# A quarter of each expert's down weights multiplied in f32 from the raw buffer, in a mixture-of-experts layer

## The reference, cut to what matters

```
gu    = xblk @ w_gu[e] + b_gu[e]          # w_gu[e]: 1024 x 2048, f32
x_glu = min(gu[:, :F], 7);  x_lin = clip(gu[:, F:], -7, 7)
act   = x_glu * sigmoid(1.702 * x_glu) * (x_lin + 1)
y     = act @ w_down[e] + b_down[e]       # w_down[e]: 1024 x 1024, f32
```

## Time and profile before

| | us |
|---|---|
| median of 3 runs | 1267.36 (1266.95 to 1268.4) |
| the profiled execution | 1267.78 |
| its span in the trace | 1266.0 |
| PE busy | 1160.1 (92%) |
| DVE busy | 1128.3 (89%) |
| ACT busy | 924.4 (73%) |
| POOL busy | 509.2 (40%) |

### The profile page before, as it was taken

One profiled execution on the slowest core, in us unless ns is written; L12 is line 12 of the kernel. 1 busy time (PEld: TensorE's weight loads), 2 busy tenths in 40 slices (PEclk: granted clock), 3 DMA queues, 4 the chain that ended last, 5 costly groups with the idle time before them and its releaser, 6 DMA issues.

```text
span 1266.0 us, 39786 instructions
## 1 busy us (share of the span) xinstructions
PE 1160.1 (92%) x17462; PEld 894.8 (71%) x17463; DVE 1128.3 (89%) x849; ACT 924.4 (73%) x819; POOL 509.2 (40%) x69
## 2 busy tenths in 40 slices
PE   5999999789999999999999999999999999999984
PEld 2455544777777777777777777777888777777741
DVE  5742454789999999999999999999999999999988
ACT  5332432579888888888888888888888888888852
POOL 0120300006666666666665551111166666622400
PEclk9999999799999999999999999999999999999998
DMA  9609331699999999999999999999999999999986
GB/s 350 218 20 353 126 134 58 229 371 378 420 416 416 418 413 417 418 418 417 416 417 414 419 418 418 414 418 413 415 416 419 417 411 420 418 412 409 418 324 255
DMA packets 73254, 458.07 MB, mean 362 GB/s; under 512 B 10076, under 2 KB 10588, under 8 KB 23632
## 3 DMA queue, kind: packets, MB, share of 16 engines
q1 hardware_dynamic: 68480, 445.30, 86.5%
q0 software_dynamic: 3472, 8.21, 1.7%
q10 hardware_dynamic: 1152, 2.19, 0.5%
HBM read 443.26 MB, written 24.77 MB: 370 GB/s over the span
## 4 chain that ended last, share of the span: by engine, by line
PE 44%; DVE 29%; issue 17%; DMA 6%; ACT 2%; DVEq 0%; SPq 0%; ACTq 0%; POOLq 0%
DVE ring L399 20%; PE ps L420 15%; PE ps L456 10%; PE ps L1093 8%; PE ps L1194 4%; PE ps L413 3%; DMA ring<-in_w_down_dram 2%; DMA arena<-in_w_down_dram 1%; DVE arena L492 1%; ACT ring L396 1%; DVE arena L486 1%; DVE arena L489 1%; DMA ring<-in_w_gu_dram 1%; DVE arena L501 1%; DVE arena L495 1%
## 5 line engine op out<-in xcount | busy, mean ns | idle before, releaser
L478 POOL DMA_INDIRECT planes<-arena,slot_row x31 | 484.2, 15619 | 586.8 <-ACT arena L508 586.8
L399 DVE SCALAR_TENSOR_TENSOR ring<-ring 128x2048 f16<-128x2048 f32 x290 | 657.5, 2315 | 15.0 <-ACT ring L396 14.7
L396 ACT ACTIVATE ring<-ring 128x2048 f16<-128x2048 f32 x290 | 543.1, 1905 | 46.4 <-DMA ring<-in_w_gu_dram 22.9
L420 PE MATMUL ps<-arena,ring 128*128 128x88 f16 x12288 | 505.1, 205 | 46.2 <-issue 27.8
L420 PEld LDWEIGHTS ps<-arena,ring 128*128 128x128 f16 x12288 | 489.2, 100 | 55.9 <-issue 43.2
L456 PE MATMUL ps<-ring,arena 128*88 128x512 f16 x1536 | 338.0, 379 | 5.6 <-DVE arena L501 2.6
L456 PEld LDWEIGHTS ps<-ring,arena 128*88 128x88 f16 x1536 | 181.4, 120 | 148.6 <-issue 6.0
L399 DVE SCALAR_TENSOR_TENSOR ring<-arena,ring 128x2048 f16<-128x2048 f32 x94 | 214.4, 2316 | 0.9 <-ACT ring L396 0.9
L396 ACT ACTIVATE ring<-arena 128x2048 f16<-128x2048 f32 x94 | 178.0, 1904 | 12.4 <-DMA arena<-in_w_down_dram 6.5
L413 PE MATMUL ps<-arena 128*128 128x88 f16 x2048 | 94.2, 207 | 10.9 <-issue 7.6
L413 PEld LDWEIGHTS ps<-arena 128*128 128x128 f16 x2048 | 86.6, 101 | 12.0 <-issue 11.9
(11 more groups left out here) (153 smaller groups left out, 592.7 us busy)
## 6 DMA issues: line engine op xcount, KB each, us to landing
ring<-in_w_gu_dram SPq DMA_DIRECT2D x194, 1024.0 KB, 11.9
ring<-in_w_down_dram SPq DMA_DIRECT2D x96, 1024.0 KB, 12.1
arena<-in_w_gu_dram SPq DMA_DIRECT2D x62, 1024.0 KB, 12.5
arena<-in_w_down_dram SPq DMA_DIRECT2D x32, 1024.0 KB, 11.7
ring<-in_w_in_dram SPq DMA_DIRECT2D x4, 2048.0 KB, 12.4
ring<-planes SPq DMA_DIRECT2D x6, 1024.0 KB, 10.1
ring<-in_w_out_dram SPq DMA_DIRECT2D x2, 2048.0 KB, 8.5
arena<-in_x_dram SPq DMA_DIRECT2D x4, 512.0 KB, 11.6
```

The source lines that it names most:

```text
L396: return act.activation(split_of(slot)[:, 0, :], raw(r), ACT.Copy, scale=SCALE_W)
L399: return dve.scalar_tensor_tensor(split_of(slot)[:, 1, :], raw(r), SCALE_W, split_of(slot)[:, 0, :], ALU.mult, ALU.subtract)
L420: mm = pe.matmul(o, w[:, i, cols], src[:, j, k, :], start=start and n == 0, stop=stop and n == 2, skip_group_check=True)
L478: return pool.indirect_dma_start(out=planes, out_offset=bass.IndirectOffsetOnAxis(ap=rows, axis=0), in_=y_row[0:SCAT, :], in_offset=None, ...
```

## The change

Chunk 8 of a stage, which is the first quarter of the down weights, is no longer split, except in stage 0 (`unsplit`), which has no expert before it and whose chunk 8 belongs to w_gu. ACT and DVE skip it. PE multiplies it in f32 from the raw buffer: 4 matmuls of 512 columns in place of 12 in f16. The activation for it is a new f32 tile `nat` (128 x 176) that ACT writes behind the high part of the activation. The raw buffer of chunk 8 is free only when PE has used it: SP waits on `chunk_used` ahead of the load into it, which is that of chunk 4 of the next stage. All other loads still wait on `low_ready`, whose counts are renumbered (`splits`). The wait on `act_ready` moves from ahead of chunk 8 to ahead of chunk 9.

```
+        nat = sb("nat", [P, 2 * CAP])
+        nat_ready = sem("nat_ready")
...
+        def unsplit(h, q, c):
+            return c == GU_CH and not (isinstance(h, int) and h == 0 and q == 0)
+
+        def splits(s, c):
+            if isinstance(s, int) and s == 0:
+                return c - DN_CH + 1
+            return (CH - 1) * s + c - DN_CH + 2 - (1 if c >= GU_CH else 0)
+
+        def raw_free(eng, h, q, c):
+            s = 2 * h + q
+            if c == GU_CH + SLOTS - CH and not (isinstance(s, int) and s == 1):
+                eng.wait_ge(chunk_used, nth(s, c) - SLOTS + 1)
+            elif c >= SLOTS:
+                eng.wait_ge(low_ready, splits(s, c - SLOTS))
+            else:
+                eng.wait_ge(low_ready, splits(s - 1, c + CH - SLOTS))
...
+        def pe_down_native(pe, r, f):
+            for half in range(2):
+                col = (f % 2) * D + half * 512
+                mm = pe.matmul(ROWS[:, half, :], nat[:, f * CAP:(f + 1) * CAP], raw(r)[:, col:col + 512],
+                               start=f == 0, stop=False, skip_group_check=True)
+            return mm
...
+        def act_nat(act):
+            return act.activation(nat[:, :], gub[:, 0, 1, :], ACT.Copy, scale=SCALE_W)
...
# SP, chunk
-                    sp.wait_ge(low_ready, nth(s, c) - SLOTS + 1)
+                    raw_free(sp, h, q, c)
...
# ACT, high
+                if unsplit(h, q, c):
+                    return
...
# ACT, act_high_part
                 act_ah(act).then_inc(ah_ready, 1)
+                if not (isinstance(e, int) and e == E - 1):
+                    act_nat(act).then_inc(nat_ready, 1)
...
# PE, down
+                if unsplit(s // 2, s % 2, c):
+                    r = raw_slot(s // 2, s % 2, c)
+                    pe.wait_ge(nat_ready, s)
+                    pe.wait_ge(slot_loaded[r], loaded(s // 2, s % 2, c))
+                    for f in range(2):
+                        mm = pe_down_native(pe, r, f)
+                    mm.then_inc(chunk_used, 1)
+                    return
+                pe.wait_ge(act_ready, s)
+                pe.wait_ge(low_ready, splits(s, c))
...
# PE, stage
-                pe.wait_ge(act_ready, s)
                 for j in range(DN_CH):
                     down(s, j, GU_CH + j)
...
# DVE, low
+                if unsplit(h, q, c):
+                    return
-                dve.wait_ge(high_ready, nth(2 * h + q, c) + 1)
+                dve.wait_ge(high_ready, splits(2 * h + q, c))
...
# DVE, taken
                     dve.wait_ge(act_ready, e)
+                    dve.wait_ge(nat_ready, e)
```

More of the change, by code:

```diff
@@ L625, in _ @@
                 slot = raw_slot(E // 2, 0, j)
-                sp.wait_ge(low_ready, nth(E, j) - SLOTS + 1)
+                raw_free(sp, E // 2, 0, j)
                 load_dn(sp, j, E - 1, slot).then_inc(slot_loaded[slot], 16)
@@ L631, in last_split @@
             def last_split():
-                sp.wait_ge(low_ready, CH * E)
+                sp.wait_ge(low_ready, splits(E, DN_CH - 1))
             def one(e, b, n):
@@ L652, in rest @@
                     t, k = i // 2, 2 * (i % 2)
-                    sp.wait_ge(low_ready, nth(E, DN_CH + i) - SLOTS + 1)
+                    raw_free(sp, E // 2, 0, DN_CH + i)
                     src = planes.rearrange("(k t p) d -> t p k d", k=TOP_K, t=NT)[t, :, k:k + 2, :]
@@ L1251, in gate_up @@
             def gate_up(s, q, k, c):
-                pe.wait_ge(low_ready, nth(s, c) + 1)
+                pe.wait_ge(low_ready, splits(s, c))
                 for b in range(GB):
@@ L1310, in _ @@
             pe.wait_ge(xT_ready, 5)
-            pe.wait_ge(act_ready, 1)
             for j in range(DN_CH):
@@ L1328, in _ @@
             pe.wait_ge(row_ready, 2 * E - 2)
-            pe.wait_ge(act_ready, E)
             for j in range(DN_CH):
```

## The result

The kernel after takes 1292.49 us (median of 4 runs, 1287.23 to 1298.28) against 1267.15 (1266.92 to 1268.4). The ratio is 1.020 with a 95% interval of 1.017 to 1.023: slower by 25 us, where 1274 was forecast. The profiled execution took 1291.9 us, its span is 1290.1.

A forecast was written before the change was run, and what follows sets the result against it. The prediction saw DVE, DMA and PE all near 30.91 us a stage, with DMA's floor about 31.2. It summed 1267.78 + 4 (start) + 3 (late PE gaps) = 1274.8, forecast as 1274, range 1260 to 1292.

The forecast's parts named there:

- PE binds throughout: Rival for all stages: PE's work with two full instruction-wait gaps, 31.85 in place of 30.91 us, +27, 1294; chance 0.13.
- both gaps: Two PE issue waits in one stage, 0.92 + 1.05 = 1.97 us, taken as waits for the next block of instructions.
- DVE's 2.20 us a stage: DVE loses one chunk a stage, 2.20 us; no gain was forecast, since the load was what came late next.
- The f32 product costs 0.85 us a stage: On PE in chunk 8: four f32 matmuls take 3.44 us where 12 f16 ones took 2.59, 0.85 more.
- ACT's copy costs nothing: ACT's new copy to `nat`, between nothing and 0.784 us, taken as 0 since ACT also loses a chunk.
- The moved wait: PE's `act_ready` wait, one chunk later than before, taken as 0 because it is met long ahead of chunk 8.
- The start, +4 us: After stage 1, SP's wait for chunk 8's buffer makes DMA lose 3.1 to 5.5 us; 4 taken.
- With the whole 0.65 in 14 stages it is 9.1 us, with none 0; I take a third, 3 us: Late stages: PE with both gaps exceeds 31.2 us by up to 0.65 in about the last 14; 3 us taken.
- the walk: Shift of the issue gaps from stage to stage: 6 matmuls before, fewer after, so the gaps come later in the run.
- the floor: DMA's time for one stage's loads, about 31.2 us, read from growing landing times and expected unchanged.
- SP's hold, taken as 0 for a steady stage: SP waits 8.6 us longer for chunk 8's buffer; loads under way cover it: 0, up to 1 us a stage for the range.
- DMA running dry once a stage: A sign, in the middle of the run, that the prediction named as proving it wrong.

## Why the prediction was wrong

The sign held, the mechanism in part, the size didn't: +25 us where +7 was forecast, 1292.49 where the range ended at 1292. The number of the rival "PE binds throughout" (1294) came, but not what it said: it had both gaps and 31.85 us in every stage, and measured are 31.17 us in eleven stages with one gap and 32.32 in the sixteen after them. That the mean is 31.85 is luck. By the prediction's steps:

- DVE's 2.20 us a stage buy nothing, since the load is next: right, and shown by the kernel that has only this relief (ratio 1.0003).
- The f32 product costs 0.85 us a stage: right, 0.87 measured.
- ACT's copy costs nothing: it is also in the kernel with only the relief, which is not slower. The moved wait was not tested by itself; no row speaks against its 0.
- The start, +4 us: DMA was dry from about 278 to 287 as said (0.58, 0.01, 0.56 in three windows). With the f16 product the hold costs 2.5 us in all, somewhat under the 3.1 to 5.5 of this step. In the kernel after it never reached PE: stage 3 begins at 323.36 us against 323.23, and stages 3 to 13 take the same time.
- "With the whole 0.65 in 14 stages it is 9.1 us, with none 0; I take a third, 3 us": this step failed. It took that PE's excess over 31.2 us would be at most 0.65 us and would shrink where SP stands. The places were right: the walk is 3.5 matmuls a stage in place of 6, the second gap arrives in stage 14 in place of stage 9, and 16 of the last 17 stages have both, where about 14 were expected. But the gaps didn't shrink: 35.2 us in stages 14 to 29, 2.20 a stage, against the 1.97 of the earlier trace rows. A late stage takes 32.32 us, 1.1 over the floor. The step also counted from 31.2, while the late stages of the kernel before took 30.76: (32.32 - 30.76) x 16 = 25.0 us.
- SP's hold, taken as 0 for a steady stage: wrong in this kernel, and the second step that failed. It costs 9 us with the f32 product (1292.5 against 1283.1), and stages 14 to 29 have 33 gaps with it and 25 without, 35.2 us against 24.2. The prediction also said that DMA running dry once a stage would make it wrong; it nearly does (135 GB/s in 724 to 726).

Why the hold brings more and longer gaps is open. A burst of loads follows each release, and the fetches may wait behind it. That fits, and in stages 14 to 29 a fetch starts 3.8 us after its border with the hold and 3.6 without (medians), but no run varied the burst alone. The comparison with and without hold shows the size only.

The whole effect, then: in the early stages PE waited for DVE before, 7.3 us in stages 3 to 13 (waits over half a microsecond). These waits are gone after, and make room for 0.66 of the 0.87 us a stage that the f32 product takes; the stages don't grow. In the late ones 0.87 us for the product and (35.2 - 17.9) / 16 = 1.08 us more of gaps come, and 0.38 us of waits for DVE go: 1.57 us a stage, where 1.56 was measured.

The chain of the earlier trace rows had said so. PE stood in it for a whole stage with 1.97 us of gaps and reached 31.0 us, 0.2 under the floor. Adding 0.85 to it gives 31.85, and that number should have been the forecast for every stage with two gaps; it was discounted by a relief of which no row spoke. For 16 stages it makes (31.85 - 30.91) x 16 = 15 us (an estimate), and 15.5 is what the kernel without the hold took more than the one before. The other 9 are the hold's.

## What to carry to other kernels

When several resources stand within 1% of each other, price a shift of work on the one that receives it, stall time included, and don't discount a stall that the trace shows. A buffer that is freed by the end of the pipeline instead of its beginning can cost more than the work that it saves: here 2.5 to 9 us, for a relief that was worth nothing. Where a transfer floor binds, look for the stretch in which the queue runs dry; filling it came out at the end almost in full.

## What the runs showed of the hardware

PE's unrolled stream stalls at places exactly 128 matmuls with their 128 weight loads apart, mostly 0.7 to 1.6 us each, while DMA is saturated. At half loads (209 to 237 GB/s over 100 us) one stall of over half a microsecond is left in 28 stages. The fetches are packets of 16.4 KB, and a stall ends about 1.4 us after one has landed. A stage has some 1030 instructions, so the places walk through the stage by a few matmuls each time. They stall PE almost only in the matmuls of 88 columns (240 in 9.4 us) and not in those of 512 (36 in 7.8 us), and whether one or two fall into this fast part decides 1 us of 32. Moving all borders by 128 instructions changed a run by 9 us with no change in its work otherwise. So two versions of such a kernel that differ in the length of their instruction stream can differ by 0.7% through this alone.

The runs of the kernel in which PE sets the pace spread over 11 us (1287.23 to 1298.28). Those of the kernel before spread over 1.5 (1266.92 to 1268.4) beside them, and over 4.6 in a set of 19 (1265.34 to 1269.94).

The f32 matmul of 512 columns with 88 weight columns took the same time as that with 128: 3.47 us for four, against 3.44.
